# Gate/up weights of an expert layer moved in sixteen 1 MB slots, each with its own wait, instead of eight 2 MB pairs

## The reference

```python
logits = t @ router_w + router_b          # 256 tokens, 32 experts
top_val, top_idx = lax.top_k(logits, 4);  gates = softmax(top_val)
for each expert e, for its tokens xe:
    g, u = split(xe @ w_gu[e] + b_gu[e])  # w_gu[e]: 1024 x 2048, 8 MB
    act  = (clip(u) + 1) * (min(g, 7) * sigmoid(1.702 * g))
    y    = act @ w_down[e] + b_down[e]    # w_down[e]: 1024 x 1024, 4 MB
    out[tokens] += gate * y
```

## Time and profile before

| | us |
|---|---|
| median of three runs (1302.84 to 1306.96) | 1303.31 |
| the profiled execution | 1303.1 |
| its span, first to last instruction | 1301.4 |
| PE busy | 1252.5 (96%) |
| PEld busy | 531.2 (41%) |
| DVE busy | 604.6 (46%) |
| SP's DMA queue, share of 16 engines | 88.7% |
| read from HBM | 476.1 MB, of it 256 MB (268.4 million bytes) w_gu and half as much w_down |

### The profile page before, as it was taken

How to read it: one execution, slowest core, us unless ns; L and a number is a source line. 1 busy time by engine, 2 the same in 40 slices (tenths; PEclk the granted TensorE clock), 3 DMA queues, 4 the chain that set the end, 5 groups by cost and what they waited for, 6 DMA issues and landing times.

```text
span 1301.4 us, 16466 instructions
## 1 busy us (share of the span) xinstructions
PE 1252.5 (96%) x5713; PEld 531.2 (41%) x5714; DVE 604.6 (46%) x1279; ACT 185.1 (14%) x390; POOL 14.1 (1%) x31
## 2 busy tenths in 40 slices
PE   6999999999999999999999999999999999899997
PEld 4867865444443333333333333333333333333332
DVE  3354698877354344343333433443443443344444
ACT  2102323431121000011000000110000111011002
POOL 0000000110000000000000000000000000000000
PEclk9999999999999999999999999999999999999999
DMA  9967665335889999999999999999999999799994
GB/s 353 339 234 281 233 236 180 130 130 223 360 321 420 428 427 428 429 430 428 428 428 428 429 428 429 428 428 429 428 429 429 428 429 429 321 428 431 428 429 207
DMA packets 59182, 477.52 MB, mean 367 GB/s; under 512 B 4991, under 2 KB 5076, under 8 KB 32532
## 3 DMA queue, kind: packets, MB, share of 16 engines
q1 hardware_dynamic: 58852, 476.11, 88.7%
q10 hardware_dynamic: 304, 1.06, 0.2%
HBM read 476.10 MB, written 1.05 MB: 367 GB/s over the span
## 4 chain that ended last, share of the span: by engine, by line
PE 73%; DMA 21%; DVE 3%; issue 1%; SPq 0%; ACT 0%; DVEq 0%; POOL 0%; ACTq 0%
PE bank L1925 23%; DMA down_ring<-in_w_down 18%; PE bank L1964 15%; PE bank L1758 7%; PE bank L1522 6%; PE bank L1557 4%; PE bank L1913 3%; PE bank L1891 3%; DMA gu_ring<-in_w_gu 3%; PE bank L1613 2%; PE bank L1814 2%; PE bank L1883 2%; DVE scratch L1337 1%; DVE scratch L1339 1%; DMA down_ring<-in_w_ada 1%
## 5 line engine op out<-in xcount | busy, mean ns | idle before, releaser
L1925 PE MATMUL bank<-gu_ring,scratch 128*64 128x512 f32 x2048 | 459.5, 595 | 1.3 <-DMA gu_ring<-in_w_gu 0.9
L1925 PEld LDWEIGHTS bank<-gu_ring,scratch 128*64 128x64 f32 x2048 | 143.2, 137 | 284.8 <-issue 282.9
L1964 PE MATMUL bank<-down_ring,scratch 128*64 128x512 f32 x1024 | 233.8, 598 | 23.1 <-DMA down_ring<-in_w_down 18.0
L1964 PEld LDWEIGHTS bank<-down_ring,scratch 128*64 128x64 f32 x1024 | 70.5, 136 | 144.3 <-issue 132.4
L1327 DVE TENSOR_TENSOR scratch<-bank,bgu 128x512 f32<-128x512 f32 x32 | 22.1, 691 | 220.4 <-PE bank L1891 220.4
L742 ACT ACTIVATE scratch<-bank 128x512 f32<-128x512 f32 x32 | 19.1, 597 | 682.5 <-PE bank L1925 682.5
L1295 DVE TENSOR_TENSOR xres<-xres,bank 128x512 f32<-128x512 f32 x132 | 81.8, 681 | 58.2 <-PE bank L1913 58.2
L1522 PE MATMUL bank<-gu_ring 128*128 128x256 f32 x384 | 84.8, 380 | 0.0
L1263 DVE TENSOR_TENSOR scratch<-bank,a 128x256 f32<-128x256 f32 x66 | 27.7, 420 | 114.3 <-PE bank L1891 114.3
L1522 PEld LDWEIGHTS bank<-gu_ring 128*128 128x128 f32 x384 | 72.4, 190 | 11.5 <-issue 1.3
L1891 PEld LDWEIGHTS bank<-ident,scratch 128*128 128x128 f32 x392 | 41.1, 140 | 80.2 <-issue 26.7
(11 more groups left out here) (285 smaller groups left out, 957.5 us busy)
## 6 DMA issues: line engine op xcount, KB each, us to landing
gu_ring<-in_w_gu SPq DMA_DIRECT2D x128, 2048.0 KB, 24.5
down_ring<-in_w_down SPq DMA_DIRECT2D x64, 2048.0 KB, 17.8
gu_ring<-in_w_in SPq DMA_DIRECT2D x32, 1024.0 KB, 8.8
gu_ring<-in_w_ada SPq DMA_DIRECT2D x16, 1024.0 KB, 7.1
down_ring<-in_w_ada SPq DMA_DIRECT2D x8, 512.0 KB, 10.3
gu_ring<-in_w_ada SPq DMA_DIRECT2D x8, 512.0 KB, 11.4
gu_ring<-in_w_pa SPq DMA_DIRECT2D x4, 1024.0 KB, 8.4
gu_ring<-in_w_pb SPq DMA_DIRECT2D x4, 1024.0 KB, 8.3
```

Source lines behind the costliest of these rows:

```text
L1925: last = M(bank[f // 2][64 * a:64 * a + 64, :], xT[:, kt % 4, kt // 4, :], gu_ring[:, 8 * half + kt, f * 512:(f + 1) * 512], start=kt == 0 ...
L1964: last = M(bank[7][64 * a:64 * a + 64, :], act_sb[:, kt % 4, kt // 4, :], down_ring[:, kt // 2, (kt % 2) * D + a * 512:(kt % 2) * D + (a + ...
```

## The change

`load_gu` calls a new `load_gu_slot` twice. This moves one slot, 1 MB: the destination is one slot, the source every second row of the block, so a partition's piece is 8 KB and its neighbour lies 16 KB further on. Each transfer signals its own slot's semaphore; the semaphores of the odd slots, which the gate/up loads did not use before, count from zero with what the table `USES` has for them. In `load_gu_pair` SP waits for each slot by itself: for kt it wants `gu_used >= item*8 + kt - 15`, where the pair wanted the count of its odd slot. TensorE waits ahead of every kt for that slot's semaphore. The w_down loads stay as they are. The order of the transfers in memory addresses and slots is the same.

```diff
         def _(sp):
             def load_gu(expert, half, j):
-                first = 8 * half + 2 * j
-                sp.dma_start(gu_ring[:, first:first + 2, :].rearrange("p r n -> p (r n)"),
-                             w_gu[0, bass.ds(expert, 1), j * 2 * P:(j + 1) * 2 * P, :]
-                             .rearrange("a (p r) n -> p (a r n)", r=2)).then_inc(slot_in[first], 16)
+                for r in range(2):
+                    load_gu_slot(expert, half, 2 * j + r)
+
+            def load_gu_slot(expert, half, kt):
+                slot, j, r = 8 * half + kt, kt // 2, kt % 2
+                rows_ = w_gu[0, bass.ds(expert, 1), j * 2 * P:(j + 1) * 2 * P, :].rearrange("a (p r) n -> p (a r) n", r=2)
+                sp.dma_start(gu_ring[:, slot, :], rows_[:, r, :]).then_inc(slot_in[slot], 16)
...
-                sp.wait_ge(gu_used, item * 8 + (2 * j - 14))
-                if j == 0:
-                    sp.wait_ge(f_gu_done, passes_made)
-                load_gu(item, half, j)
+                for kt in (2 * j, 2 * j + 1):
+                    sp.wait_ge(gu_used, item * 8 + (kt - 15))
+                    if kt == 0:
+                        sp.wait_ge(f_gu_done, passes_made)
+                    load_gu_slot(item, half, kt)
...
                     if kt == KT // 2:
                         pe.wait_ge(xTe_late, item + 1)
-                    if kt % 2 == 0:
-                        pe.wait_ge(slot_in[8 * half + kt], fills * 16 + 16 * USES[8 * half + kt])
+                    pe.wait_ge(slot_in[8 * half + kt], fills * 16 + 16 * USES[8 * half + kt])
```

## The result

The changed kernel takes 1310.96 us (median of 7 runs, 1309.0 to 1315.34) against 1303.63 us for the kernel before (7 runs, 1302.84 to 1307.89). The ratio is 1.0053, with a 95% interval from 1.0041 to 1.0064: 5.3 to 8.3 us slower, 6.9 at the middle. The prediction said +3.0 and a range up to 1310.2, so the sign and the main term were right and the size was not. Of the rivals, A (1308.8, the early gain fails) has what happened; B's 1310.8 is nearer by number, but by luck, for its cost of 0.12 us a pair did not come (0.071 was measured). The profiled execution of the changed kernel took 1310.96 us with a span of 1309.2 (before 1303.1 and 1301.4).

What follows compares the result with a forecast made beforehand. The weights' DMA stream was taken to bound the kernel until item 25's last gate/up landing, TensorE's work alone after it. +6.4 - 2.6 - 0.9, with 0.1 for TensorE's start, gave +3.0: 1306.3 us, range 1301.8 to 1310.2.

Steps and rivals of the forecast that it cites:

- A: Rival: the early gain at item 2 fails, w_down's release or slow first packets holding the stream; 1308.8 us, chance 0.24.
- B: Rival: packets cost more in strided reads of alternate rows, 0.12 us a pair; 1310.8 us, chance 0.11.
- Part 1: Gate/up stream to item 25: 8 KB pieces and a semaphore a megabyte add 0.070 us a pair, +6.4 us.
- the packet estimate: Cost from 2 KB pieces' rates: 9 ns a packet, so 81 ns for a gate/up pair's added packets and semaphore.
- rival D: Each added gate/up transfer pays its fixed part as in an empty queue, 2.4 us, about 440 us more; chance 0.01.
- Rival C: The stream keeps its rate, 8 KB pieces meeting the same ceiling as 16 KB ones; 1300.4 us, chance 0.10.
- Part 2: SP's waits by slot land item 2's last gate/up 2.6 us earlier, and item 1's w_down keeps up.
- the sum 1.7 + 1.2: Item 2's gate/up: first slot leaves 1.7 us earlier, and a hole at the third pair, 1.2 us, is filled.
- it just does: Item 1's first w_down half, released at 398.32 us, keeps up with the stream, which wants it at about 399.5.
- Part 3: TensorE's waits by slot: already met ones cost nothing; at item 25 gate products run before the last slot, -0.9 us.
- Part 4: Issuing an item's eight gate/up transfers takes 4.5 us instead of 2.1, covered by the queue, also at the restart.
- Part 5: TensorE still sets the end: item 31's last gate/up keeps 1.0 us of its 1.5 to spare; no new wait.

Runs made afterwards that it cites:

- e1_one_dma_8k: Changed kernel with 2 MB gate/up transfers again, four an item, each of two alternating slots in 8 KB pieces; 1314.94 us, 1.0081 against the kernel before.
- e2_sp_pair_wait: Changed kernel, but SP waits for both slots of a pair before issuing their two 1 MB transfers; 1310.02 us, 1.0045 against the kernel before.
- e3_pe_pair_wait: Changed kernel, but TensorE waits for both slots of a pair ahead of each even contraction step; 1311.73 us, 1.0047 against the kernel before.
- e5_pairs_26_31: Changed kernel, but items 26 to 31 load gate/up in 2 MB transfers of 16 KB pieces; 1311.37 us, 1.0046 against the kernel before.
- e10_down1_by_slot: Changed kernel, but item 1's first w_down half moves in two 1 MB transfers, the first issued earlier; 1311.42 us, 1.0054 against the kernel before.
- e7_late_down1: Changed kernel with one more SP wait ahead of item 1's w_down, issued 0.57 us later; one run, w_down landed 0.30 us later than in the changed kernel.
- e11_both: Gate/up by slot only for item 2 and item 25's last pair, 16 KB pairs elsewhere, item 1's first w_down half split; 1305.31 us, 0.9998 against kernel before.

## Where the prediction was right and where it was wrong

**Part 1, the stream's cost: right.** +0.070 us a pair was forecast, 6.55/92 = 0.0712 measured. The interval forecast at 29.65 is 29.69. It rested on the row of the same form, four loads of w_ada; the packet estimate of 9 ns, from the 2 KB rows, was as good, as the curve shows. The mechanism is now shown and not just argued: the pieces pay, the transfers do not. By rival D's rule each of the 184 would have paid 2.4 us; e1_one_dma_8k, with half the transfers, has the interval of the kernel after to 0.01 us (29.682, 29.690). Rival C (the rate is kept) and rival B (0.12 us a pair) are out.

**Part 2, SP's waits by slot: this is the step that failed.** 2.6 us were forecast at item 2's last gate/up, to be kept by w_down; two steps of this were wrong. The first is the sum 1.7 + 1.2. The first slot left 1.7 earlier (3.69 - 1.98 = 1.71), but the text carried this to the last slot without asking when the third could leave. It left at S + 7.48 and landed 4.35 us behind the second, and at the end of pair 1 the lead was 0.03. The 1.2 for a second hole at the third pair did come: 1.12 of the 1.15 at the last slot arise there. Then came what the text called "it just does": item 1's w_down. I had it issued in time at S + 23.5 with 7.7 to 9.7 us to land, and took the gain as kept. It took 10.3, so the gain of 1.15 turned into a loss of 0.59, and at the second half +0.57. My own lower end ("the release decides, gain 0 to 2") named the mechanism, but its price came from a load into an empty queue and from the same load behind a full one, and the case between, a queue just running out, was slower than both. Of the +0.57 at the second half, 0.37 goes with SP's waits by slot, since e2_sp_pair_wait without them has +0.20 (S + 38.26). Instead of -2.6 the part gives +0.6, a miss of 3.2 us, and that is nearly all of the error of the sum: -2.6 against +0.57, with +6.55 and -0.81 as forecast within 0.15. e2_sp_pair_wait, without these waits, is as fast as the kernel after: the part is worth nothing.

**Part 3, TensorE's waits by slot: right.** -0.9 was forecast, -0.81 measured from the landing to the end. Waits that are already met cost nothing that shows: 27.37 to 27.38 us an item in both kernels. Not foreseen was that the wait at item 25 is also short, 0.56 us, and that the kernel so escapes the half clock that e3_pe_pair_wait met behind 2.09 us.

**Part 4, issuing: right.** At the restart behind the further pass the eight issues of an item take 4.4 us (4.5 forecast), and in the full stream e1_one_dma_8k, with half as many transfers, has the same interval.

**Part 5, the end: right.** Item 31's last slot landed at 1282.10 and was wanted at 1282.87, 0.8 us of slack, where 1.0 was forecast; TensorE waits for no weights behind item 25, and e5_pairs_26_31 gains nothing.

**What is left.** The terms of the change sum to +6.31 us (forecast +3.0). The profiles differ by 7.8, of which 1.52 is the clock's draw in the token mixer. The ratio's interval, 5.3 to 8.3, holds both, so the runs do not tell whether the medians have some of that draw in them too. The range was too short at its upper end for that reason: A's 1308.8 has 1.4 us to the bound, while the draw alone moves an execution by 1.5.

**Still open.** Why w_down takes 10.3 us to land behind a queue that runs out. Both things are there: the release (first megabyte issued 1.6 us earlier in e10_down1_by_slot, worth 0.7; all of it 0.6 later in e7_late_down1, costing 0.3) and single 16 KB pieces that take up to 1.5 us, where most take 0.61. The engines' idle time there, 0.25 us on average, is the smaller part, but how the 1.7 us divides between a late release and slow pieces was not separated, nor why single pieces are slow. Nor is it known why e11_both lands w_down 1.3 us earlier than e10_down1_by_slot. The dip is gone in both, with the release alone changed (418 to 438 GB/s from 402 to 410 us in e10_down1_by_slot), and up to there both issue the same transfers; 0.7 of the 1.3 lie already in the last gate/up slot, 26.76 and 27.48. The kernel after and two others with its start agree at w_down within 0.12 us (33.72, 33.64, 33.60), but each is one profile. Why the early gain of these two kernels shrinks by 0.4 to 0.5 us between the w_down of item 3 and of item 4 is open too; the DMA share is 1.01 there.

## What to carry to other kernels

Where one stream of weights sets the pace, price the pieces and not the transfers: count pieces on each DMA engine, times about 10 ns; splitting a transfer cost nothing that shows here, splitting its rows did. A finer wait gains only if the next thing in the queue can follow, so a forecast gain has to be carried from release to release, with each load's landing time taken from a queue in the same state. And follow an early gain to the place where it is to pay, at the semaphore that the consumer really waits for: in e11_both it was 1.45 us at item 1's first w_down half and gone at item 25.

## What the runs showed of the hardware

- A piece costs a DMA engine 9.5 to 10.3 ns besides its bytes, the same from 4 to 32 KB; four transfers more an item don't show (29.690 and 29.682 us, with 0.045 us between kernels of the same transfers).
- A load issued while the queue runs out lands later than one into an empty queue: 10.3 us for 2 MB against 7.7, and 7.3 us for a 1 MB slot against 5.1 for the first slot of item 2.
- Behind a wait of TensorE of 2.2 us in the kernel after (at 861 us) and one of 2.09 in e3_pe_pair_wait (at 1097) the granted clock fell to 0.50, the level of 1.2 GHz, for some 3.4 us; behind the wait of 0.56 it did not. It cost only where TensorE had no slack behind it: about 1.7 us there, and nothing seen in the kernel after, which waits for w_down again further on.
- One wait and one signal more in the w_down product cost TensorE 0.10 us an item (27.47 for 27.37), while four waits more hung on gate/up matmuls cost none (27.37).
